# Masking by two extra contraction rows and by an expanded bias, with bias addition and row maximum in one vector pass

## The reference

```python
# layer 0, query block of 128, 256 keys, chunks of 64
s = jnp.einsum('bqhd,bkhd->bhqk', qblk, k) * scale
mask = kchunk[None, :] <= qchunk[:, None]
s = jnp.where(mask[None, None], s, neg)
p = jax.nn.softmax(s, axis=-1)
# layer 1, query chunk of 64, its own chunk and 8 before it
s = jnp.einsum('bqhd,bkhd->bhqk', qch, kb) * scale + bias[None]
s = jnp.where(valid[None, None, None, :], s, neg)
p = jax.nn.softmax(s, axis=-1)
```

## Time and profile before

| | |
|---|---|
| median of 3 runs | 1549.7 us (1549.39 to 1551.93) |
| span of the profiled execution | 1548.5 us |
| PE busy | 1473.5 us, 95% |
| DVE busy | 1158.8 us, 75% |
| ACT busy | 951.1 us, 61% |
| POOL busy | 43.0 us, 3% |
| chain that ended last, by engine | PE 92%, DVE 4%, ACT 2%, issue 1% |

### The profile page before, as it was taken

The page is one execution under the profiler, slowest core; times in us unless marked ns, Lnnn a source line. Parts: engine busy times, 40 slices in busy tenths (PEclk is TensorE's granted clock), DMA queues, the critical chain, the costliest instruction groups (busy, mean ns, idle before and its releaser), DMA issues.

```text
span 1548.5 us, 20274 instructions
## 1 busy us (share of the span) xinstructions
PE 1473.5 (95%) x7313; PEld 1220.3 (79%) x7313; DVE 1158.8 (75%) x1033; ACT 951.1 (61%) x919; POOL 43.0 (3%) x79
## 2 busy tenths in 40 slices
PE   5788999998987899999999999999999999999998
PEld 5577999997876688788878878878887887887885
DVE  4665544456684888888888888888888888888884
ACT  4454443335453567767676777776676767666672
POOL 3120000000000000000000000000000000000000
PEclk9889999999999999999999999999999999999999
DMA  8323455554622599989989999999998998999992
GB/s 295 121 86 130 142 190 178 179 186 136 216 83 82 190 338 370 358 308 372 368 291 369 373 319 340 371 326 328 380 357 306 367 371 296 368 366 326 342 365 81
DMA packets 226273, 424.65 MB, mean 274 GB/s; under 512 B 7981, under 2 KB 38842, under 8 KB 226234
## 3 DMA queue, kind: packets, MB, share of 16 engines
q1 hardware_dynamic: 218272, 417.23, 76.4%
q10 hardware_dynamic: 7578, 6.84, 1.5%
q0 software_dynamic: 384, 0.07, 0.1%
HBM read 423.06 MB, written 4.19 MB: 276 GB/s over the span
## 4 chain that ended last, share of the span: by engine, by line
PE 92%; DVE 4%; ACT 2%; issue 1%; POOL 0%; DMA 0%; ACTq 0%; POOLq 0%; SPq 0%; DVEq 0%
PE ps L1305 81%; PE ps L1300 3%; PE ps L1629 2%; PE ps L1603 2%; PE ps L1419 2%; PE ps L1441 1%; DVE wl_a L873 1%; ACT wh_a L557 0%; ACT tn L566 0%; DMA xr<-in_x 0%; DVE htl L892 0%; DVE kT L1001 0%; DVE nmax L1014 0%; DVE bias L1011 0%; POOL rstd L449 0%
## 5 line engine op out<-in xcount | busy, mean ns | idle before, releaser
L873 DVE TENSOR_TENSOR wl_a<-raw,wh_a 128x2048 fp32r<-128x2048 f32 (+1 forms) x230 | 513.6, 2268 | 115.6 <-ACT wh_a L557 115.6
L557 ACT ACTIVATE wh_a<-raw 128x2048 fp32r<-128x2048 f32 (+1 forms) x230 | 430.5, 1899 | 168.4 <-PE ps L1305 167.9
L873 DVE TENSOR_TENSOR wl_b<-raw,wh_b 128x2048 fp32r<-128x2048 f32 x168 | 380.3, 2287 | 85.6 <-ACT wh_b L557 85.5
L557 ACT ACTIVATE wh_b<-raw 128x2048 fp32r<-128x2048 f32 x168 | 316.7, 1918 | 40.8 <-PE ps L1305 40.8
L1305 PE MATMUL ps<-wh_a,hth 128*128 128x512 f32 (+2 forms) x608 | 245.4, 404 | 6.2 <-DVE htl L892 3.5
L1305 PE MATMUL ps<-wh_a,htl 128*128 128x512 f32 (+2 forms) x608 | 237.0, 390 | 0.0
L1305 PE MATMUL ps<-wl_a,hth 128*128 128x512 f32 (+2 forms) x608 | 236.2, 388 | 0.0
L817 ACT ACTIVATE gth<-ps 128x512 fp32r<-128x512 f32 x56 | 33.5, 597 | 227.7 <-PE ps L1300 227.7
L1305 PE MATMUL ps<-wh_b,htl 128*128 128x512 f32 x416 | 164.9, 396 | 0.0
L1305 PE MATMUL ps<-wl_b,hth 128*128 128x512 f32 x416 | 164.8, 396 | 0.0
L1305 PE MATMUL ps<-wh_b,hth 128*128 128x512 f32 x416 | 164.7, 396 | 0.0
(11 more groups left out here) (233 smaller groups left out, 2058.8 us busy)
## 6 DMA issues: line engine op xcount, KB each, us to landing
raw<-in_moe_w SPq DMA_DIRECT2D x336, 1024.0 KB, 7.0
raw<-in_ffn_w SPq DMA_DIRECT2D x33, 1024.0 KB, 5.3
raw<-in_a_w_o SPq DMA_DIRECT2D x4, 1024.0 KB, 6.2
raw<-in_b_w_q SPq DMA_DIRECT2D x4, 1024.0 KB, 5.1
raw<-in_kv_w_k SPq DMA_DIRECT2D x4, 1024.0 KB, 5.1
raw<-in_kv_w_v SPq DMA_DIRECT2D x4, 1024.0 KB, 5.0
raw<-in_b_w_o SPq DMA_DIRECT2D x4, 1024.0 KB, 5.0
bias<-bias_wide ACTq DMA_DIRECT2D x8, 384.0 KB, 3.2
```

The source lines that it names most:

```text
L557: nc.scalar.activation(dst[:, 0:w], raw[:, n % RAW, 0:w], ACT.Copy).then_inc(hi_done, 1)
L873: nc.vector.tensor_tensor(l[:, 0:w], raw[:, n % RAW, 0:w], h[:, 0:w].bitcast(fp32), ALU.subtract).then_inc(lo_done, 1)
```

## The change

In attention one the mask is no longer a product of its own. The tiles `qT` and `kT` get two rows more, 96 and 97, and the contraction runs over 98 rows instead of 96: row `r` of `qT` is 1 for the first 64 queries of tile `r`, row `r` of `kT` is -2^100 for the last 64 keys that this tile can see. The rows are constants; SP writes them once, with 8 small DMAs, which wait until PE has used the last unit of the key and value expansion (the tiles lie over buffers of that stage), and which stand in SP's list ahead of the first weights of the dense layer. PE waits for them (`mask_here`) ahead of the first scores. The constant `mask` tile and its copy on ACT are gone.

In attention two the mask stands in `bias_wide`: the expansion now takes six DMAs, two of which write -2^100 where the first 64 queries meet the last 64 keys. The addition and the maxima become `tensor_tensor_reduce`: it writes -(scores + bias) and takes the minimum of that, once for the 128 and once for the 256 columns. The exponential uses the scale -1. The wait for `sb` is gone; the bank is free when the maxima are done. DVE's loop over the middle pairs is written out in attention two.

```diff
+            sp.wait_ge(unit_used, U_UKV + 2)
+            for tile_, at in ((qT, C_MA), (kT, C_MB - CHUNK)):
+                for r in range(T):
+                    for t in range(T):
+                        dst = tile_[QK + r:QK + r + 1, :, :].rearrange("p a (h t q) -> p (a h) t q", h=2, t=T)[:, :, t, :]
+                        row = 0 if r == t else 1
+                        sp.dma_start(dst, consts[row:row + 1, at:at + P].unsqueeze(1).to_broadcast([1, 4, P])).then_inc(mask_here, 16)
...
-            nc.scalar.activation(mask[:], cst[:, C_MA:C_MA + P + CHUNK], ACT.Copy).then_inc(mask_done, 1)
...
                         last = nc.scalar.activation(prob[:, par, h, lo_:lo_ + n_], src[:, lo_:lo_ + n_], ACT.Exp,
+                                                    scale=1.0 if la == 0 else -1.0,
...
             for at, skip, keys in ((0, P, P), (P, 0, SEQ)):
-                src = bass.AP(tensor=bias_rows.tensor, offset=P - 1 + skip, ap=[[SPAN, HEADS], [-1, P], [1, keys]])
-                act.dma_start(bias_wide[:, :, at:at + keys], src).then_inc(wide_done, 16)
+                for q0, seen in ((0, keys - CHUNK), (CHUNK, keys)):
+                    src = bass.AP(tensor=bias_rows.tensor, offset=P - 1 + skip - q0, ap=[[SPAN, HEADS], [-1, CHUNK], [1, seen]])
+                    act.dma_start(bias_wide[:, q0:q0 + CHUNK, at:at + seen], src).then_inc(wide_done, 16)
+                act.dma_start(bias_wide[:, 0:CHUNK, at + keys - CHUNK:at + keys],
+                              bass.AP(tensor=consts.tensor, offset=C_MB,
+                                      ap=[[0, HEADS], [0, CHUNK], [1, CHUNK]])).then_inc(wide_done, 16)
...
-                        src = bias[:, par, h, :]
-                        nc.vector.tensor_tensor(src, ps[2 + h][:, 0:SPAN], src, ALU.add).then_inc(a["sb"], 1)
-                        dve.wait_ge(a["sb"], p * 2 + (h + 1))
...
+                            b = bias[:, par, h, lo_:lo_ + n_]
+                            last = nc.vector.tensor_tensor_reduce(b, src[:, lo_:lo_ + n_], b, -1.0, 3e38, ALU.add, ALU.min,
+                                                                  nmax[:, par, t, h:h + 1])
...
-                        pe.wait_ge(a["ex" if la == 0 else "sb"], p * 2 + (h - 1))
+                        pe.wait_ge(a["ex" if la == 0 else "nm"], p * 2 + (h - 1))
...
-                        mm(ps[2 + h][:, lo_:lo_ + keys], qT[part, par, q_at + t * P:q_at + (t + 1) * P],
-                           kT[part, par, h * SEQ:h * SEQ + keys], start=True, stop=False)
-                        last = mm(ps[2 + h][:, lo_ + keys - CHUNK:lo_ + keys], mask_row, mask_col, start=False, stop=True)
+                        last = mm(ps[2 + h][:, lo_:lo_ + keys], qT[part, par, q_at + t * P:q_at + (t + 1) * P],
+                                  kT[part, par, h * SEQ:h * SEQ + keys], start=True, stop=True)
```

More of the change, by code:

```diff
@@ L126, in trunk_kernel @@
         ropt = sb("ropt", [P, 2, 2, T, ROPE])
-        mask = sb("mask", [P, P + CHUNK], f32r)
         negh = sb("negh", [P, T])
@@ L214, in trunk_kernel @@
         number = cst[:, C_E3:C_E3 + V_EXTRA * NE].rearrange("p (i e) -> p i e", e=NE)
-        mask_row = mask[:, 0:P]
-        mask_col = mask[:, P:P + CHUNK]
         q1 = q_all[:, :, 0:D]
@@ L234, in trunk_kernel @@
         c_here = sem("c_here")
-        mask_done = sem("mask_done")
+        mask_here = sem("mask_here")
         g_here = sem("g_here")
@@ L277, in trunk_kernel @@
                 "s",
-                "sb",
                 "nm",
@@ L685, in attention @@
                 if la == 1:
-                    act.wait_ge(wide_done, 32)
+                    act.wait_ge(wide_done, 16 * 6)
                     load_bias(0, 0, wait=False)
@@ L1006, in maxima @@
                     src = ps[2 + h]
-                    if la == 1:
-                        if h == 0:
-                            dve.wait_ge(bias_here[par], (p - par) * 8 + 16)
-                        src = bias[:, par, h, :]
-                        nc.vector.tensor_tensor(src, ps[2 + h][:, 0:SPAN], src, ALU.add).then_inc(a["sb"], 1)
-                        dve.wait_ge(a["sb"], p * 2 + (h + 1))
-                    for t, (lo_, n_) in enumerate(((0, P), (P, SEQ))):
-                        last = nc.vector.tensor_reduce(nmax[:, par, t, h:h + 1], src[:, lo_:lo_ + n_], axis=AX,
-                                                       op=ALU.max, negate=True)
+                    if la == 1 and h == 0:
+                        dve.wait_ge(bias_here[par], (p - par) * 8 + 16)
+                    for t, (lo_, n_) in enumerate(((0, P), (P, SEQ))):
+                        if la == 0:
+                            last = nc.vector.tensor_reduce(nmax[:, par, t, h:h + 1], src[:, lo_:lo_ + n_], axis=AX,
+                                                           op=ALU.max, negate=True)
+                        else:
+                            b = bias[:, par, h, lo_:lo_ + n_]
+                            last = nc.vector.tensor_tensor_reduce(b, src[:, lo_:lo_ + n_], b, -1.0, 3e38, ALU.add, ALU.min,
+                                                                  nmax[:, par, t, h:h + 1])
                     last.then_inc(a["nm"], 1)
@@ L1052, in attention @@
                 step(1, 1)
-                with dve.Fori(1, PAIRS // 2 - 1) as j:
-                    for u in range(2):
-                        step(j * 2 + u, u)
+                if la == 0:
+                    with dve.Fori(1, PAIRS // 2 - 1) as j:
+                        for u in range(2):
+                            step(j * 2 + u, u)
+                else:
+                    for p in range(2, PAIRS - 2):
+                        step(p, p % 2)
                 step(PAIRS - 2, 0, more=False)
@@ L1448, in attention @@
                 yield
-                pe.wait_ge(mask_done, 1)
+                if la == 0:
+                    pe.wait_ge(mask_here, 16 * 8)
                 scores(0, 0, 0, first=True)
```

2 lines of the change are left out of this document (1 added, 1 removed).

## The result

The changed kernel is slower, by 0.6%. Its median is 1560.3 us (4 runs, 1559.21 to 1561.52), beside 1550.8 us for the kernel before in the same session (4 runs); the ratio is 1.0063, with a 95% interval of 1.0048 to 1.0077. The prediction was 1539.5, faster. The profiled execution has a span of 1557.4 us against 1548.5, so 8.9 us are to be explained.

A forecast was written before the change was run, and what follows sets the result against it. PE was taken to pace the experts, chains of waits over PE and DVE the attentions. Gains of 4.0 (attention one) and 6.2 (attention two), 10.2 together, off 1549.7 gave 1539.5 us, range 1537.0 to 1545.0.

The forecast's parts named there:

- the expansion of the bias on ACT: Ahead of attention one: six DMA issues take 3.9 us, hidden within 4.19 before the turned queries, so no cost.
- Rival (b): Ahead of attention one: ACT's six issues, at 1.28 each, are not hidden; 3.5 us back, 1543.0; chance 0.08.
- the upper bound of 7.7: Expansion on ACT: six issues at the dearer seen price, 1.28 each, take 7.7 us; attention one starts 3.5 later.
- The eight small DMAs on SP: Ahead of attention one: eight issues at 0.39, 3.1 us, out by 72.2, needed at 85; cost nothing.
- Attention one: Dropping four mask products per pair, 0.11 us each at full clock, cuts the period from 4.81 to 4.37; gain 4.0.
- rival (c): Start of attention one: PE's clock rises later, half of about 3.5 us is lost, 1.7; 1541.2; chance 0.06.
- Attention two: Masks (0.44) and a shorter vector pass (0.34) cut the period from 5.26 to 4.48; eight pairs gain 6.2 us.
- the lower bound of 0.54: Attention two's vector pass per head, if accumulator readings cost nothing and passes overlap: 0.54 us instead of the forecast 0.78.
- (a): Attention two: the vector pass stays at 1.12 us, readings eating the gain; total gain 6.1, 1543.6; chance 0.13.
- (d): Attention two: the new vector instruction is expensive, 2.0 us a head; eight pairs lose 12.0, 1557.7; chance 0.04.
- DVE's branch: Attention two: second chain, 2.76 us plus two passes, 4.32 in all; said to be longer from a pass of 0.96.
- (e): Experts: the gain is lost later because DMA, not PE, leads there; 1549.7, the same time; chance 0.05.

The follow-up runs named there:

- before_sixq: The kernel before with its two expansion DMAs on ACT cut by queries (43, 43, 42) into six, still 4096 rows: 1552.5 us, ratio 1.0010.
- rows16_early: rows16 with SP's first two loads of the dense layer issued ahead of its wait for the mask rows: 1544.4 us, ratio 0.9963.
- rows16: The changed kernel with its two constant DMAs reading 16 different rows, one per head, instead of one address: 1546.9 us, ratio 0.9974.
- rows64: The changed kernel with its two constant DMAs reading 64 different rows, each 16 times, instead of one address: 1546.1 us, ratio 0.9972.
- merged: The changed kernel with its two constant DMAs reading 1024 different rows, 80 elements apart: 1546.2 us in one profiled run.
- before_three: The kernel before with the wide half of the expansion cut by keys, giving three DMAs and 6144 rows: 1555.4 us, ratio 1.0028.
- const_last: The changed kernel with its four bias DMAs issued first and the two constant DMAs, still reading one place, last: 1550.1 us in one profiled run.
- pass_only: The kernel before with only the vector pass of attention two changed, masks and expansion as before: 1546.8 us, ratio 0.9975.
- on_sp: The changed kernel with its six expansion DMAs issued by SP instead of ACT, the constant's one-address source kept: 1542.3 us, ratio 0.9950.

## Why the prediction was wrong

**The failed step** is the expansion of the bias on ACT: "I take 3.9, hidden with 0.3 to spare". It took 22.9 and the lead grew by 17.92. As a price for a free queue the 0.65 per DMA came out, before_sixq measured 0.67, but by luck: the slope by rows that gave it took the mean of a free issue and of one that was already held (0.70 and 1.28). Free issues took 0.65 to 0.71 whether they had 688, 1024 or 2048 rows (before_sixq, rows16_early, before). What the step left out has three parts, from the leads: 12.70 for reads of one place (20.79 - 8.09), 2.99 for the loads of SP that came together with it (8.09 - 5.10), 2.23 for 6144 rows in six DMAs (5.10 - 2.87). Rival (b) named the place and the mechanism, issues that are not hidden, and what spoke for it, a queue that pushes back; its price, 3.5, was five times too small, since it took the dearest issue seen for the dearest possible. No row of before shows a DMA that reads one place a thousand times; there the upper bound of 7.7 was no bound.

**The eight small DMAs on SP.** "Cost: nothing" holds for them: issued by 73.3 (I had 72.2; 0.6 each instead of 0.39) and nobody waits. But the sentence on what is queued behind them asked only who needs those loads, not what else the DMA engines do at that time. They fell on the expansion, 3.0 us.

**Attention one.** Forecast 4.0, measured 3.0 to 3.2: a mask product was worth 0.083 of the period (0.33 / 4), not 0.11; the lower bound in the text, 0.09, was nearer. A head without masks took 0.76 (116.78 - 116.02), where the prediction had 0.68: the 0.11 from one start to the next is more than a mask product added to the head. Where the first scores came at 88 to 90 us (rows16, rows64, merged, rows16_early) the stage is 0.4 to 0.8 longer than where they came at 83 to 85 or after 91: the clock rose later, which is rival (c) at a smaller price (its 3.5 us of lower clock stood on no row). In rows16, scores at 90.17, PEclk is 0.50 from 92 to 96 us and 0.88 from 96 to 100; in the changed kernel, scores at 101.91, it is 0.74 from 104 to 108 already. before_three shows how dear that can be: a lead 0.85 longer and the stage 3.93 longer, with PEclk at 0.51 from 96 to 100 us though PE was busy for 4.00 of 4.00.

**Attention two.** Forecast 6.2, measured 6.6, but by errors that cancel: the pass was to bring 2.7 and brings 4.56 alone (0.56 a head instead of 0.78, near the lower bound of 0.54), the masks were to bring 3.5 and bring the other 2.06. That the copy of the keys stays the link was right: PE waits 0.44 for it. Rivals (a) and (d) fall with this: the new instruction is not dear, and the rule weighed in the prediction, the Trainium skill's advice against fusing ("VectorE: DVE Perf Modes", Rules for kernel authors), would have kept the pass at 1.12; this chip took 0.56. (The pass from which DVE's branch would be the longer one is 0.94 by the prediction's own terms, not 0.96; nothing hangs on it.)

**After the attentions.** Everything passed to the end, as forecast: 1080.1 us behind attention two in both, so (e) falls. Not forecast: the clock can fall behind attention one. In seven of the 18 kernels of the table the turning took 4.02 or 4.03 instead of 2.94 (in const_last 3.77), and in others up to 2.8 us went on the way to attention two. It goes with no edit that I can name, and it differs between executions of one kernel too. Of the 71 executions of the kernel before that were timed beside the experiments, 56 have a mean granted clock of 0.983 or 0.984 and took 1548.9 to 1551.4 us; 14 have 0.979 and took 1551.5 to 1552.4; the last one, at 0.981, took 1554.8. In pass_only it is seven at 1545.4 to 1547.1 (0.982 or 0.983) and four at 1547.8 to 1548.7 (0.978). So a difference of one to three us in these two columns of the table, which rest on one execution each, cannot be put down to an edit by the table alone. Why the clock falls in one execution and not in another was not tested and stays open.

## What to carry to other kernels

A DMA issue on a computing engine's list costs what the queue makes it cost, not what an issue costs: count the rows outstanding, ask what else moves at that time, and never let a thousand rows of a DMA be read from one place: 16 rows 3840 bytes apart were enough here. A wait put into an issuing engine's list moves every transfer behind it; look where they land, even if nobody waits for them. Big scattered transfers that are needed late go to an engine that does nothing else.

## What the runs showed of the hardware

- Reads of 256 B at one place in HBM, or at places 4 bytes apart, go at 18 to 20 GB/s in total, some 72 in a us, at a DMA share of 0.07 as at 0.47; with 16 or 64 places 3840 bytes apart, or 1024 places 320 bytes apart, the lead is 8.0 to 8.1 us instead of 20.7 to 20.8.
- An issue by ACT takes 0.65 to 0.71 us while the queue is free, for 688 rows as for 2048, and 1.0 to 7.3 once it is not (up to 7.5 on SP in on_sp); the turning point lay near 4096 rows, and earlier, at the third thousand (3.92 us), when SP's 1 MB loads were in flight.
- A DMA whose outermost count is 6 or 5 moved 107 to 135 GB/s at a DMA share of 0.36 to 0.41; cut by queries, with 16 outermost, at a share of 1.07, the same bytes held ACT for 4.81 us instead of 17.87.
- On DVE, addition with a minimum took 0.21 and 0.34 us from start to start for 128 and 256 columns, and its accumulator reading overlapped fully with what followed.
- The granted clock fell from 1.00 to 0.55 within 140 to 142 us of the changed kernel, with no idle time of PE longer than 0.59 us in the eight us before; the kernel before kept 1.00 at the same place of the program.
